# Two transformer blocks on one core: MoBA key rotation in three parts, second block's keys inside the fourth feed-forward, compressed second layer over qg's first unit

## The chip, the cores and the metric

The kernel runs on one core of a Trainium2 chip. The metric is the device time of one execution in microseconds. TensorE multiplies, VectorE (DVE) and ScalarE (ACT) work on tiles, GpSimd (POOL) makes inverse roots, and SyncE (SP) issues the weights' DMAs. Each engine runs its own instructions in the order in which they were written, and waits on semaphores for the others.

## The reference, cut to what matters

The first block mixes DSA attention (indexer, top-64 keys) with MoBA attention (one block of 256 here, so plain causal attention) and a gated feed-forward. The second block has four feed-forwards, a short convolution, and NSA attention, whose keys and values are made from the stream between the two layers:

```python
k_b = apply_rope(rms_norm(k_b.reshape(B, S, MOBA_HEADS, HEAD_DIM), g_k_moba[l]), cos_h, sin_h)
...
kv = (_rmsnorm(h, kv_norm) @ kv_w).reshape(b, s, N_KV_SLOTS, N_KV_GROUPS, HEAD_DIM_2)
k_cmp = _rmsnorm(_compress(kv[0], cmp_pos[0], cmp_w1[0], cmp_b1[0], cmp_w2[0]), k_norm[0])
v_cmp = _compress(kv[1], cmp_pos[1], cmp_w1[1], cmp_b1[1], cmp_w2[1])
k_sel = _rmsnorm(kv[2], k_norm[1])...
k_win = jnp.pad(_rmsnorm(kv[4], k_norm[2]), pad)
...
def _compress(x_raw, pos, w1, b1, w2):
    ...
    return jax.nn.gelu(flat @ w1 + b1) @ w2
```

There are 256 tokens, a model width of 1024, and everything is float32.

## The kernel before

**Weights.** All weight matrices are cut into units of 128 x 2048 words. A ring of three slots takes them from memory. ScalarE rounds a unit into its high half (`w_hi`, L926, and L1216 inside a feed-forward), VectorE subtracts for the low half (`w_lo`, L1264, which also frees the raw slot for the next DMA), and TensorE makes each product from three matmuls: high x high, high x low, low x high (L1741 to L1743). One part of a projection is one unit: 24 matmuls of 512 columns, two token tiles times four slices of the depth. The activations have halves too (`h_hi` L988, `h_lo` L1406), made from transposed tiles of x (L1908).

**Order.** `make_plan` writes one list of items by hand; every engine walks it and does its share of each item, so a place in the list is a place in five queues. `part(stage, chunk, number, parts, after, inside)` puts the items of `inside` between the quarters or halves of a unit's matmuls and those of `after` behind them, and then the split of the unit three further on (unless `held`). `tp` is a group of transposes into bank 6 or 7, in turn, with its copy out; `evac` takes a product out of its banks. `t_free` and `t_done` count the groups.

**First block.** The stages run qi, ki, qb, kb, vb, ga, and so on. The indexer's score goes in eight `ix` items (two matmuls at L1979, two relus on ScalarE at L1138, two scaled additions on VectorE at L1549; each waits for the one before). At the evacuation of kb, ScalarE copies and squares, and VectorE makes the tables, sums the squares (L1492), rotates both token tiles (`rope`, L1277 to L1280, four operations each) and scales by the inverse root (L1504). The item `tp kb` transposes the keys behind vb's second unit (L1914). MoBA attention runs between the quarters of ga (`qk` L1993, `sm`, transposes of the probabilities L1962, `pv`).

**Second block.** kv makes six slots in three chunks: chunk 0 for the compressed branch, chunks 1 and 2 for selected and windowed keys and values. `keys(c)` on VectorE scales the keys with root and gain and writes them twice (L1307, L1309), into `kp` and `kd`, one buffer for both chunks. `kvt` groups transpose them (L1939, copy L1032): chunk 1's in front of the fourth feed-forward, `f3`, chunk 2's between the two compressed layers. `cm` makes the hidden rows of the compressed keys and values (two units each), their evacuation is a GELU (L1115), `hc` transposes them, `cmp` multiplies by the second layer (L2007 and L2011), and `kc` transposes the compressed key. Then come qg (queries), gn (gates) and the NSA attention, in which ScalarE's exponentials (L1170) and VectorE's maxima (L1593) and scalings (L1609) pass work to TensorE pair by pair.

**Feed-forward.** `ffn` has 11 steps. A step multiplies two gate/up units, then the down unit of the step before, then transposes the gated activations. Steps 0 to 2 and 9 to 10 are written out, six run in a loop. `square` (L956) makes the norm's sums of squares.

## Time and profile before

| | |
|---|---|
| median of three runs | 1521.61 us (1521.04 to 1523.71) |
| the profiled execution | 1521.8 us, span 1519.8 us |
| TensorE busy | 1465.2 us, 96% |
| VectorE busy | 851.5 us, 56% |
| ScalarE busy | 689.8 us, 45% |
| DMA, mean | 178 GB/s, q1 at 53.6% of 16 engines |
| mean granted TensorE clock | 0.987 |

The page gives the busy time of each engine over the whole span. The timeline gives, for each group of equal instructions, its start, its length, and in brackets how long its engine stood idle before it and what ended that. The windows view adds the granted TensorE clock of a stretch, as a share of 2.4 GHz. Matmuls overlap, so a distance between two starts prices them better than their length.

### The profile page before, as it was taken

Reading aid. Unit: us, or ns where it says so; the run is one execution under the profiler, and the core shown is the slowest. Engines: PE = TensorE matmul, PEld = TensorE weight load, DVE = VectorE, ACT = ScalarE, POOL = GpSimd, SP = SyncE. Lnnn points to the kernel's source line nnn. Section 1 sums busy time; section 2 is a strip of 40 time slices with the busy share of each in tenths; the row PEclk is TensorE's granted clock in tenths of the full one; section 3 lists DMA queues with packets and bytes.
Section 4 is the critical chain, followed back from the end, with each engine's and each line's share of the span. In section 5 each row is a group of like instructions: output and inputs, shape, how many; then the busy total and the mean of one; then the engine's idle time right before and its main releaser. Section 6 shows DMA issues by size and latency. Waiting matters only on the chain.

```text
span 1519.8 us, 18042 instructions
## 1 busy us (share of the span) xinstructions
PE 1465.2 (96%) x6944; PEld 1168.5 (77%) x6944; DVE 851.5 (56%) x1032; ACT 689.8 (45%) x875; POOL 37.4 (2%) x53
## 2 busy tenths in 40 slices
PE   6989999999999999999999999989999988999998
PEld 3747777788888888888888888778888765788887
DVE  2676765555446544456755545565554567654453
ACT  2535453443344444454453444654344575554432
POOL 0010100000000000000000000210000020000000
PEclk9999999999999999999999999999999998999999
DMA  9853754465554665546555555555556430355562
GB/s 339 284 188 111 253 190 166 166 203 188 190 194 138 222 193 178 183 159 202 192 175 185 193 186 174 146 186 191 179 191 193 145 111 1 95 183 192 176 192 77
DMA packets 187880, 270.11 MB, mean 178 GB/s; under 512 B 8350, under 2 KB 134118, under 8 KB 187816
## 3 DMA queue, kind: packets, MB, share of 16 engines
q1 hardware_dynamic: 186448, 267.01, 53.6%
q10 hardware_dynamic: 1208, 1.94, 0.4%
q0 software_dynamic: 160, 0.26, 0.2%
q8 instruction: 44, 0.72, 0.2%
q14 instruction: 20, 0.16, 0.0%
HBM read 268.15 MB, written 1.05 MB: 177 GB/s over the span
## 4 chain that ended last, share of the span: by engine, by line
PE 85%; DVE 6%; ACT 4%; DMA 2%; issue 2%; SPq 1%; POOL 0%; ACTq 0%; DVEq 0%
PE bank L1741 25%; PE bank L1743 25%; PE bank L1742 25%; DVE w_lo_ring L1264 2%; PE bank L1771 2%; ACT w_hi_ring L926 2%; PE bank L1879 1%; DMA arena<-in_w_mod_dram 1%; PE bank L1908 1%; PE bank L2063 1%; PE bank L1966 1%; DMA raw_ring<-in_w_in_dram 1%; SPq L830 0%; PE bank L2042 0%; DVE h_lo L1406 0%
## 5 line engine op out<-in xcount | busy, mean ns | idle before, releaser
L1264 DVE TENSOR_TENSOR w_lo_ring<-raw_ring,w_hi_ring 128x2048 fp32r<-128x2048 f32 (+1 forms) x228 | 518.4, 2277 | 420.3 <-ACT w_hi_ring L1216 332.4
L1741 PE MATMUL bank<-w_hi_ring,h_hi 128*128 128x512 f32 x1360 | 544.6, 400 | 6.1 <-DVE h_lo L1406 3.1
L1743 PE MATMUL bank<-w_hi_ring,h_lo 128*128 128x512 f32 x1360 | 532.4, 391 | 0.0
L1742 PE MATMUL bank<-w_lo_ring,h_hi 128*128 128x512 f32 x1360 | 532.1, 391 | 0.0
L1216 ACT ACTIVATE w_hi_ring<-raw_ring 128x2048 fp32r<-128x2048 f32 x158 | 302.8, 1916 | 295.8 <-PE bank L1743 293.6
L1741 PEld LDWEIGHTS bank<-w_hi_ring,h_hi 128*128 128x128 f32 x1360 | 256.6, 189 | 75.8 <-issue 24.6
L1743 PEld LDWEIGHTS bank<-w_hi_ring,h_lo 128*128 128x128 f32 x1360 | 256.5, 189 | 55.4
L1742 PEld LDWEIGHTS bank<-w_lo_ring,h_hi 128*128 128x128 f32 x1360 | 257.0, 189 | 49.7
L1741 PE MATMUL bank<-w_hi_ring,f_hi 128*128 128x512 f32 (+1 forms) x456 | 177.4, 389 | 0.0
L1743 PE MATMUL bank<-w_hi_ring,f_lo 128*128 128x512 f32 (+1 forms) x456 | 176.5, 387 | 0.0
L1742 PE MATMUL bank<-w_lo_ring,f_hi 128*128 128x512 f32 (+1 forms) x456 | 176.2, 386 | 0.0
L926 ACT ACTIVATE w_hi_ring<-raw_ring 128x2048 fp32r<-128x2048 f32 (+2 forms) x70 | 131.1, 1879 | 84.4 <-PE bank L1743 41.5
L1224 ACT ACTIVATE glu_s<-bank,rstd 128x256 f32<-128x256 f32 x88 | 36.9, 471 | 142.0 <-PE bank L1743 142.0
L1741 PEld LDWEIGHTS bank<-w_hi_ring,f_hi 128*128 128x128 f32 (+1 forms) x456 | 85.0, 186 | 17.9 <-issue 1.1
L1743 PEld LDWEIGHTS bank<-w_hi_ring,f_lo 128*128 128x128 f32 (+1 forms) x456 | 85.0, 186 | 17.3
L1742 PEld LDWEIGHTS bank<-w_lo_ring,f_hi 128*128 128x128 f32 (+1 forms) x456 | 85.1, 187 | 16.8
L1691 DVE SCALAR_TENSOR_TENSOR glu_a<-bank,rstd,glu_s 128x256 f32<-128x256 f32 x88 | 38.5, 479 | 64.8 <-ACT glu_s L1224 64.8
L1697 DVE TENSOR_TENSOR f_lo<-bank,f_hi 128x512 fp32r<-128x512 f32 x55 | 37.6, 685 | 10.3 <-ACT f_hi L1230 10.3
L1230 ACT ACTIVATE f_hi<-bank 128x512 fp32r<-128x512 f32 x55 | 32.0, 582 | 20.9 <-PE bank L1771 20.9
L1170 ACT ACTIVATE arena<-bank,mn,arena 128x128 f32<-128x128 f32 (+1 forms) x64 | 31.9, 518 | 10.8 <-DVE mn L1596 10.6
L988 ACT ACTIVATE h_hi<-bank,cols 128x256 fp32r<-128x256 f32 x56 | 21.9, 475 | 31.7 <-PE bank L1908 31.7
L1771 PE MATMUL bank<-const,glu_a 128*128 128x128 f32 x236 | 35.3, 271 | 0.0
(254 smaller groups left out, 881.7 us busy)
## 6 DMA issues: line engine op xcount, KB each, us to landing
raw_ring<-in_ffn_w_gate_up_dram SPq DMA_DIRECT2D x176, 512.0 KB
raw_ring<-in_ffn_w_down_dram SPq DMA_DIRECT2D x44, 1024.0 KB
raw_ring<-in_w_in_dram SPq DMA_DIRECT2D x22, 1024.0 KB
raw_ring<-in_w_gate_up_dram SPq DMA_DIRECT2D x44, 512.0 KB
arena<-in_w_mod_dram SPq DMA_DIRECT2D x12, 1024.0 KB, 7.8
raw_ring<-in_w_mod_dram SPq DMA_DIRECT2D x12, 1024.0 KB
raw_ring<-in_w_down_dram SPq DMA_DIRECT2D x11, 1024.0 KB
raw_ring<-in_conv_w_in_dram SPq DMA_DIRECT2D x16, 512.0 KB
```

The source lines that it names most:

```text
L926: act.activation(w_hi[:, u % RING, 0:words], raw[:, r % RING, 0:words], ACT.Copy)\
L1170: ins = act.activation(p_n[:, step % 2, 2 * j + br, 0:n], bank[j][:, br * n:br * n + n], ACT.Exp, scale=rqp[:, qt, h:h + 1], bias=mn[:, c: ...
L1216: act.activation(w_hi[:, u % RING, :], raw[:, unit_raw[u] % RING, :], ACT.Copy)\
L1224: act.activation(glu_s[:, tt, :], glu_bank(f, jb, tt)[:, 0:GC], ACT.Silu, scale=rstd[:, tt:tt + 1] if f else 1.0).then_inc(sem("sg_ready"), 1)
L1230: act.activation(f_hi[:, jb % 2, :, :].rearrange("p a b -> p (a b)"), bank[6 + tg % 2][:, :], ACT.Copy).then_inc(sem("hi_t"), 1)
L1264: dve.tensor_tensor(w_lo[:, u % RING, 0:words], raw[:, r % RING, 0:words], w_hi[:, u % RING, 0:words].bitcast(F32), ALU.subtract).then_inc ...
L1691: dve.scalar_tensor_tensor(glu_a[:, tt, :], glu_bank(f, jb, tt)[:, GC:2 * GC], rstd[:, tt:tt + 1] if f else 1.0, glu_s[:, tt, :], ALU.mult ...
L1697: dve.tensor_tensor(f_lo[:, jb % 2, :, :].rearrange("p a b -> p (a b)"), bank[6 + tg % 2][:, :], f_hi[:, jb % 2, :, :].rearrange("p a b -> ...
L1741: pe.matmul(dst, hi, whi, start=start, stop=False)
L1742: pe.matmul(dst, hi, wlo, start=False, stop=False)
L1743: return pe.matmul(dst, lo, whi, start=False, stop=stop)
L1771: ins = pe.transpose(bank[6 + tg % 2][:, kk * T + tt * P:kk * T + (tt + 1) * P], glu_a[:, tt, kk * P:(kk + 1) * P], ident)
```

## The change

**MoBA keys.** At the evacuation of kb VectorE now only makes the tables and sums the squares. The rest is in three new items, `rot` for each token tile and `rot scale`, which stand inside vb: behind the last quarter of its first unit (after `ix` 5), behind the first quarter of its second unit, and behind its last quarter. The index items move back by a quarter where needed, and `tp kb` moves into ga, behind its first quarter.

**Keys of the second block.** `kp` and `kd` get a second buffer each. `keys(1)` moves from the evacuation of kv 1 to step 0 of `f3`, ahead of `keys(2)`. The four groups of key transposes stand in step 2 of `f3`, two between its gate/up units and two behind them, and ScalarE's copies stand ahead of and behind its silu. The evacuation of kv 2 waits for the sums of squares of kv 1 in place of the keys.

**Compressed branch.** The second layer of the compressed keys (`cmp` 0), their root and transposes, and the second layer of the values stand between the quarters of qg's first unit; the squares of the norm come behind that unit. The split that followed qg's second unit stands behind gn's evacuation and two query copies, ahead of the gates' transposes.

```diff
-        part("gn", 0, 0, 1, [evac("gn"), tgroup("qn", 2, c=0), one("tp", stage="gnt", g=0)])
+        part("gn", 0, 0, 1, [evac("gn"), tgroup("qn", 2, c=0), one("then split", unit=len(units) - 1), one("tp", stage="gnt", g=0)])
...
-    part("vb", 0, 0, 2, [mod_row(6, 1)], [index[3], [], index[4], index[5]])
-    part("vb", 0, 1, 2, [mod_sum(6), tgroup("kb", 2), evac("vb")], [index[6], [], index[7], []])
+    rot = [[dict(kind="rot", tt=tt)] for tt in range(TT)] + [[dict(kind="rot scale")]]
+    part("vb", 0, 0, 2, [mod_row(6, 1)], [[], index[3], index[4], index[5] + rot[0]])
+    part("vb", 0, 1, 2, [mod_sum(6), evac("vb")], [rot[1], index[6], index[7], rot[2]])
...
-    part("ga", 0, 0, 2, [topk(0, 0)], inside[0])
+    part("ga", 0, 0, 2, [topk(0, 0)], [tgroup("kb", 2) + inside[0][0]] + inside[0][1:])
...
-    begin_glu("f3", 6, FIRST_PAIR[3], tgroup("norm", 4, norm=6)[2:] + [dict(kind="square")] + kvt(1, 2))
+    begin_glu("f3", 6, FIRST_PAIR[3], tgroup("norm", 4, norm=6)[2:] + [dict(kind="square")])
...
-    part("cm", 0, 1, 2, [kvt(2, 2), evac("cm", 0)])
-    part("cm", 1, 0, 2, [[dict(kind="square")]])
-    part("cm", 1, 1, 2, [evac("cm", 1)], [[dict(kind="tp", stage="hc", g=0, c=0), dict(kind="cmp", s=0)], []])
-    part("qg", 0, 0, 2, inside=[[dict(kind="tp", stage="kc", g=0), dict(kind="tp", stage="hc", g=0, c=1)], [],
-                                [dict(kind="cmp", s=1)], []])
-    part("qg", 0, 1, 2, [evac("qg", 0)])
+    part("cm", 0, 1, 2, [evac("cm", 0)])
+    part("cm", 1, 0, 2)
+    part("cm", 1, 1, 2, [evac("cm", 1)], [[dict(kind="tp", stage="hc", g=0, c=0)], []])
+    part("qg", 0, 0, 2, [[dict(kind="square")]], [[dict(kind="cmp", s=0)], [dict(kind="tp", stage="hc", g=0, c=1)],
+                                                  [dict(kind="tp", stage="kc", g=0)], [dict(kind="cmp", s=1)]])
+    part("qg", 0, 1, 2, [evac("qg", 0)], held=True)
...
+        kps = (kp, carve(TT, 256))
+        kds = (kd, kv_d_flat[:, 0:1024].rearrange("p (t g u d) -> p t g u d", t=TT, g=NG, u=2))
...
-                            act.wait_ge(sem("kd_done"), 1)
+                            act.wait_ge(sem("qss_ready"), item["nq"])
...
+                        def key_copies(c):
+                            for a in item["keys"] if jb == 2 else ():
+                                if a["c"] == c:
+                                    act.wait_ge(sem("t_done"), a["tg"] + 1)
+                                    act.activation(kn_t[:, c - 1, 2 * a["g"]:2 * a["g"] + 2, :].rearrange("p a b -> p (a b)"),
+                                                   bank[6 + a["tg"] % 2][:, :], ACT.Copy).then_inc(sem(f"t_free{a['tg'] % 2}"), 1)
...
-                        if c == 1:
-                            keys(c)
...
+                if k == "rot":
+                    tt = item["tt"]
+                    dve.wait_ge(sem("t_done"), find["tg", "qb", 1] + 1)
+                    rope(ro[:, tt, :], pq[:, tt, :], tab_c[:, tt, :], tab_s[:, tt, :], NH, HD)
+                if k == "rot scale":
+                    dve.wait_ge(sem("qr_ready"), key_nq + 1)
...
-                            (lambda: keys(2), compressed_operand, lambda: compressed_operand_lo(0))[j]()
+                            (lambda: (keys(1), keys(2)), compressed_operand, lambda: compressed_operand_lo(0))[j]()
...
+                    def key_transposes(c):
+
+                        for a in item["keys"]:
+                            if a["c"] == c:
+                                wait_bank(pe, a["tg"])
+                                pe.wait_ge(sem("kd_done"), c)
+                                for kk in range(2):
+                                    for tt in range(TT):
+                                        at = T * kk + P * tt
+                                        ins = pe.transpose(bank[6 + a["tg"] % 2][:, at:at + P],
+                                                           kds[c - 1][:, tt, 2 * a["g"] + kk, :, :].rearrange("p a b -> p (a b)"), ident)
...
+                        if jb == 2:
+                            key_transposes(1)
                         glu_unit(u + 1, 1, None, two).then_inc(sem("unit_used"), 1)
+                        if jb == 2:
+                            key_transposes(2)
```

## Rows read from the trace of the kernel before

**Rows 1.** The page, busy time of each engine with its share of the span and instructions.

```profile
PE 1465.2 (96%) x6944; PEld 1168.5 (77%) x6944; DVE 851.5 (56%) x1032; ACT 689.8 (45%) x875; POOL 37.4 (2%) x53
```

**Rows 2.** The waits of TensorE: us in total, times, longest us.

```profile
PE bank L1966 <- DVE arena L1609: 3.9, 3, 1.7
```

**Rows 3.** Timeline, VectorE near 100: start, us, instruction, count, idle before.

```profile
94.12 0.68 DVE L1277 TENSOR_TENSOR glu_s<-arena 128x512 f32<-128x512 f32 x1
...
98.36 1.29 DVE L1504 TENSOR_TENSOR arena<-arena,qr 128x512 f32<-128x512 f32 x2
99.57 2.28 DVE L1264 TENSOR_TENSOR w_lo_ring<-raw_ring,w_hi_ring 128x2048 fp32r<-128x2048 f32 x1
101.77 0.80 DVE L1549 SCALAR_TENSOR_TENSOR arena<-arena 128x128 f32<-128x128 f32 x2
...
104.72 1.07 DVE L1549 SCALAR_TENSOR_TENSOR arena<-arena 128x256 f32<-128x256 f32 x2 [1.03 <-ACT arena L1138]
```

**Rows 4.** Timeline, TensorE from 100 to 124.

```profile
103.04 1.22 PE L1979 MATMUL bank<-arena 64*128 64x256 f32 x4 [5.67 <-ACT arena L1138]
...
115.27 1.07 PE L1914 MATMUL bank<-const,arena 128*128 128x128 f32 x8
...
123.06 0.30 PE L1962 MATMUL bank<-const,arena 128*128 128x128 f32 x1 [0.57 <-ACT arena L1145]
```

**Rows 5.** Windows: length, PE, PEld, DVE, ACT, POOL busy, clock, DMA share, GB/s.

```profile
97.40:103.00 5.60, 0.00 (x0) 0.00 (x0) 5.37 (x8) 0.77 (x2) 0.00 (x0) 0.88 0.01 3
103.00:108.40 5.40, 5.36 (x18) 2.53 (x18) 3.77 (x6) 2.46 (x3) 0.00 (x0) 0.50 0.58 191
...
990.00:997.00 7.00, 4.71 (x26) 3.70 (x27) 5.90 (x11) 4.49 (x8) 3.80 (x2) 1.00 0.92 309
1194.60:1198.10 3.50, 0.33 (x3) 0.19 (x2) 1.77 (x2) 3.42 (x6) 0.89 (x2) 0.90 0.23 31
1198.10:1204.40 6.30, 6.30 (x25) 5.08 (x25) 3.69 (x7) 0.79 (x3) 0.72 (x2) 0.51 0.88 296
...
1244.00:1300.00 56.00, 49.73 (x294) 32.09 (x293) 40.53 (x103) 32.56 (x111) 4.44 (x3) 0.88 0.00 1
```

**Rows 6.** Timeline, TensorE in front of the fourth feed-forward.

```profile
990.76 0.47 PE L1741 MATMUL bank<-w_hi_ring,h_hi 128*128 128x512 f32 x1 [3.13 <-DVE h_lo L1406]
...
996.04 1.44 PE L1939 MATMUL bank<-const,arena 128*128 128x128 f32 x8 [1.40 <-DVE h_lo L1406]
...
997.24 0.48 PE L1741 MATMUL bank<-w_hi_ring,h_hi 128*128 128x512 f32 x1
...
1000.08 0.39 PE L1741 MATMUL bank<-w_hi_ring,h_hi 128*128 128x512 f32 x1
```

**Rows 7.** Timeline, VectorE at kv and in step 2 of f3.

```profile
983.07 0.43 DVE L1307 TENSOR_TENSOR arena<-arena,qr 128x256 f32<-128x256 f32 x1 [2.05 <-POOL qr L861]
...
985.34 4.48 DVE L1264 TENSOR_TENSOR w_lo_ring<-raw_ring,w_hi_ring 128x2048 fp32r<-128x2048 f32 x2
...
1033.95 2.29 DVE L1264 TENSOR_TENSOR w_lo_ring<-raw_ring,w_hi_ring 128x2048 fp32r<-128x2048 f32 x1 [2.88 <-ACT w_hi_ring L1216]
```

**Rows 8.** Timeline, TensorE in the compressed branch and at gn.

```profile
1188.31 1.44 PE L1939 MATMUL bank<-const,arena 128*128 128x128 f32 x8 [0.47 <-DVE h_lo L1406]
...
1198.10 0.68 PE L2007 MATMUL bank<-arena 128*60 128x64 f32 x4 [3.18 <-ACT arena L1042]
...
1221.06 0.32 PE L1919 MATMUL bank<-const,arena 48*128 48x48 f32 x2 [1.37 <-ACT arena L1036]
```

**Rows 9.** Timeline, ScalarE behind qg's first chunk.

```profile
1218.35 1.93 ACT L926 ACTIVATE w_hi_ring<-raw_ring 128x2048 fp32r<-128x2048 f32 x1
...
1223.18 1.91 ACT L926 ACTIVATE w_hi_ring<-raw_ring 128x2048 fp32r<-128x2048 f32 x1
...
1227.58 1.28 ACT L1170 ACT_TABLE_LOAD   x1 [2.49 <-DVE arena L1585]
```

More of the change, by code:

```diff
@@ L462, in make_plan @@
             item["tg"], item["hl"], item["gi"] = number("tg", NJ), number("hl", NJ), number("gi", NJ)
+            item["keys"] = [dict(c=c, g=g, tg=item["tg"] + 2 + 2 * (c - 1) + g) for c in (1, 2) for g in range(2)] if item["f"] == 3 else []
+            number("tg", len(item["keys"]))
             for u in range(item["have"], min(item["unit"] + 3 * NJ + RING, len(units))):
@@ L728, in wait_product, with act_group @@
             eng.wait_ge(sem("unit_used"), find["unit", stage, chunk] + 1)
+        def act_group(item, jb):
+            return item["tg"] + jb + (len(item["keys"]) if jb >= 2 else 0)
         def glu_bank(f, jb, tt):
@@ L1023, in _ @@
                         act.activation(ki_t, b[:, 0:T], ACT.Copy).then_inc(free, 1)
-                    elif st == "kvt" and item["c"] == 0:
+                    elif st == "kvt":
                         s_, g0 = divmod(2 * g, NG)
@@ L1030, in _ @@
                            .then_inc(free, 1)
-                    elif st == "kvt":
-                        act.activation(kn_t[:, item["c"] - 1, 2 * g:2 * g + 2, :].rearrange("p a b -> p (a b)"),
-                                       b[:, :], ACT.Copy).then_inc(free, 1)
                     elif st == "qn":
@@ L1930, in _ @@
                     elif st == "kvt":
-                        if item["c"] == 0:
-                            wait_pair(pe, find["pi", "kv", 0])
-                            s_, g0 = divmod(2 * g, NG)
-                            srcs = [kv_d[:, tt, s_, g0 + kk, :, :] for kk in range(2) for tt in range(TT)]
-                        else:
-                            pe.wait_ge(sem("kd_done"), item["c"])
-                            srcs = [kd[:, tt, 2 * g + kk, :, :] for kk in range(2) for tt in range(TT)]
+                        wait_pair(pe, find["pi", "kv", 0])
+                        s_, g0 = divmod(2 * g, NG)
+                        srcs = [kv_d[:, tt, s_, g0 + kk, :, :] for kk in range(2) for tt in range(TT)]
                         for q, s_ in enumerate(srcs):
@@ L2104, in step @@
                             if jb == NJ - 1 and kk == 0:
-                                glu_transposes(item["tg"] + jb, item["gi"] + jb)
+                                glu_transposes(act_group(item, jb), item["gi"] + jb)
                         ins.then_inc(sem("unit_used"), 1)
                         if jb < NJ - 1:
-                            glu_transposes(item["tg"] + jb, item["gi"] + jb, two, 0 if i is None else i)
+                            glu_transposes(act_group(item, jb), item["gi"] + jb, two, 0 if i is None else i)
                     free_pairs(item)
@@ L2120, in _ @@
                     body, q = item["of"], item["q"]
-                    u, tg = body["unit"] + 3 * NJ - 1, body["tg"] + NJ - 1
+                    u, tg = body["unit"] + 3 * NJ - 1, act_group(body, NJ - 1)
                     nb, tt = divmod(q, 2)
```

37 lines of the change are left out of this document (26 added, 11 removed).

## The prediction

> **What bounds the kernel now.** Read the engine totals first: TensorE is busy 1465.2 of 1519.8 us [rows 1]. Everything else hides behind it, so an edit is worth only the TensorE idle time it removes, the half-speed time which that idle brings, and the TensorE work it adds or saves. So next comes TensorE's timeline, for its gaps, and behind each gap the queue of the engine named as releaser. Three gaps lie where the diff works.
>
> First, at 103.04 TensorE stood 5.67 us for a relu [rows 4]. VectorE explains it: from 94.12 it made the MoBA key rotation (two ropes, then the scaling at 98.36), then a weight split at 99.57, and only at 101.77 the indexer sum that lets the relu go [rows 3]. After the gap the granted clock is 0.50, that is 1.2 GHz, from 103.0 to 108.4, where it had been 2.4 GHz [rows 5]. Second, at 990.76 TensorE stood 3.13 us for h_lo, and at 996.04 again 1.40 us [rows 6]; VectorE made kv's first keys at 983.07 and behind them two splits of 4.48 us before h_lo [rows 7]. Third, at 1198.10 it stood 3.18 us for the hidden row's transposed copy [rows 8]; ScalarE was busy 3.42 of these 3.50 us with squares and a split that stand ahead of the copy, and the clock was then 0.51 to 1204.4 [rows 5].
>
> **A. Rotation in three parts.** VectorE is free at 94.1; the high half of the pending split is ready about 94.65 (ScalarE's like piece takes 1.93 [rows 9]). Its new queue: split 2.28 to 96.9; third index sum 0.80 to 97.7. The hand-off from that sum over relu to TensorE is 103.04 - 102.57 = 0.47 [rows 3, 4], so index product 5 runs at 98.2 instead of 103.04. TensorE comes to it at about 97.1 (its work ended by 97.4 [rows 5], and one wait of 0.3 on its way goes with the new order), so a wait of 1.1 remains. VectorE goes on: two index sums of 1.07 with 0.45 of hand-off, rot 2.1 (94.12 to 98.36 is two of them), a 128x512 addition 0.68, split 2.28, rot 2.1, two index sums 2.14, scaling 1.29 [rows 3]. Sum 97.7 + 13.2 = 110.9: only then may the key transposes run. TensorE's work from product 5 to the old key transposes is 115.27 - 103.04 = 12.2 [rows 4], of which 5.4 ran at half speed and so holds 2.7 [rows 5]; without that it is 9.5, and TensorE comes to ga at 107.7. The transposes now stand behind ga's first quarter, two triples of three products at 0.71 (997.24 to 1000.08 is four [rows 6]), so from 109.1 it waits 1.8. From there to the first probability transpose at 123.06 the order is the old one, with 0.57 idle that goes, since VectorE and ScalarE have their splits behind them. Work from 103.04 to 123.06: 20.0 - 0.57 - 2.7 = 16.7; new 98.2 + 16.7 + 1.8 = 116.7, gain 6.3. I take **6.0** for hand-offs unpriced. Bounds: 4 if the new wait costs a piece of low clock as the old one did and VectorE is a little late, 8.4 (5.67 + 2.7) if no wait is left.
>
> **B. kv and the fourth feed-forward.** Keys 1 leave VectorE's queue ahead of the splits (983.07 to 985.34 and the wait for the root before it). The first split can start at 981.65, when its high half is done; two splits of 2.24 end at 986.15, the first two h_lo, half of four of like size, at 987.0. TensorE ends kv at 987.5, so the 3.13 gap goes whole: 3.3 by starts. Then two runs of four triples (2.84 each) and eight transposes bring it to the first unit of the feed-forward at 994.0; there it needs the third h_lo, whose queue (evacuation of kv 2, split 2.28, h_lo 0.85) ends at 994.95. So 994.95 stands against 1000.08 [rows 6]: 5.1. What moves into step 2: 16 transposes. Eight take 1.07 busy [rows 4], of which some 0.24 lies over their neighbours (996.04 + 1.44 against 997.24); the old ones took 1.20 start to start [rows 6]. I take 0.8, so 1.6, and 2.4 as the upper bound. A TensorE transpose, per the Trainium skill (TensorE: Matmul & The Clock Gate, Part 4: PE-mode transpose), took some 275 ns in the context of one kernel; by that the 16 would cost 4.4 us and the total would be 2.8 us worse; the rows here show 0.13 busy for each and decide against it. Behind them: step 0 now carries both keys on VectorE, 2.3 more ahead of three splits; the second unit of step 1 would be split at 1022.9, needed at 1028. In step 2 ScalarE copies two key groups (1.1) before its next split. The low half of that unit ends at 1036.24 [rows 7], and would end 1.1 later; TensorE asks for it 1.6 later too, at 1041.1 in old time. The weights' DMAs are issued when the low halves are done, so at most 2.3 later once, with more than a step of cover. No loss from either, up to 3 us if this cover fails. Net **3.5** (1 to 4.3).
>
> **C. Compressed branch.** The key transposes of kv 2 leave (wait 0.47 and 1.37 start to start, with edges 2.0). The hidden row is evacuated right behind the first compressed layer, 1.4 earlier than the table load now lets it, and the squares leave the queue ahead of its copy. ScalarE: evacuation 1188.1 to 1189.75, split to 1191.6, split to 1194.1 (0.6 allowed for its weights to land), copy 1194.3; TensorE asks at 1195.75, because qg's first quarter now stands before the product. The 3.18 gap goes, and the half-speed time to 1204.4, whose 5.9 up to the next transposes hold 2.8 of loss [rows 5]. The root of the compressed key now has two qg quarters over it: sums, root and scaling, 2.1 us, end at 1199.1; TensorE asks at 1199.2. One wait of 0.25 comes in front of the second half of the second layer, for VectorE's split. 2.0 + 3.2 + 2.8 - 0.25 = **7.8**. Bounds: 5 if the clock falls anyway or the root is 1 us late, 8.5.
>
> **D. The split of qg's last unit.** It moves behind gn's evacuation and two query copies. TensorE's 1.37 wait at 1221.06 [rows 8] falls to 0.2. But the attention behind it is led by ScalarE and VectorE: exp loads its table at 1227.58 on VectorE's word, which follows the split that ScalarE ended at 1225.1 [rows 9]. Before, that stretch of ScalarE had no idle; now it waits 0.35 for gn, 0.35 for transposes, while no work leaves it. So the chain starts 0.7 later, and TensorE, though 1.2 us ahead, waits for it: three waits for the scaled probabilities make 3.9 [rows 2]. **-0.7** (+1.2 to -1.5).
>
> **Sum.** 6.0 + 3.5 + 7.8 - 0.7 = 16.6. The profiled execution took 1521.8, its span 1519.8 with 2.0 around it, and the median is 1521.6, the same within 0.2. 1521.8 - 16.6 = 1505.2; I say **1505**.
>
> **Rivals.** (1) *The waits stay, smaller, and the clock falls.* The new 1.8 in A, and 1.0 to 2.0 in front of the attention's first products, bring stretches at 1.2 GHz; the old ones in the attention bring its mean to 0.88 [rows 5]. One in A costs 1.7, one in D 1.7: 1508.5. For it: 3.18 at 1198.10 brought one. Against it: 3.13 and 1.40 at 990.76 and 996.04 brought none, the clock stayed 1.00 [rows 5]. Chance 0.2. (2) *VectorE stays late in A, or the copies hold ScalarE in step 2.* A gives 2.5 or B loses 3: 1508 to 1510. VectorE's queue from 94.65 to 110.9 has almost no air; each us more is one us less gain. Chance 0.13. (3) *The attention gets better.* 0.88 over 56 us is some 13 us at half clock, 6.7 of loss [rows 5]; a shift of the whole kernel may spare part: 4 spared, 1501. Chance 0.1. (4) *Slower.* In the attention TensorE is busy 49.73 of 56 us [rows 5]. With the chain later and TensorE ahead its waits lengthen; if the clock then stays at 1.2 GHz through the stage, each us of work costs another. It eats the gain from 33 us of wall time at half clock on, and over the whole stage costs some 40: 1545. For it, 0.88 already; against it, total work is the same and the waits grow under 2 us. Chance 0.03. The Trainium skill (TensorE: Matmul & The Clock Gate, HAM oscillation) tells of a kernel in which recurring waits throttle the array again at each tile; by that rule case 4 would come. (5) *The change doesn't move the path*, because what I call released is held by another wait: near 1520, 0.03. The forecast itself, 0.51.
>
> **Range and chances.** 1500 to 1511 holds the forecast, (1), (2) and most of (3). A measurement tells 0.2%, 3 us, from no change. Faster 0.94, same 0.03, slower 0.03.
>
> **What would show it.** In the changed profile: the wait before the fifth index product about 1 us and one of 1 to 2.5 before the key transposes; clock 1.00 at 98 to 108; no gap over 0.5 before the fourth feed-forward's first product and about 1 before its first unit; 16 more transposes in it and no gap in its steps 2 and 3; no gap over 1 and full clock in the compressed layers; the exp table load 0.7 later behind qg's evacuation than now. It is wrong if TensorE stands over 3 us at the key transposes, if step 3 waits for a split, or if the attention takes more than 2 us longer from qg's evacuation to its end.

## The result and the profile after

The changed kernel takes 1504.36 us in the median of four runs (1503.17 to 1506.15), against 1521.67 before (1521.04 to 1523.71). The ratio is 0.9888, with a 95% interval of 0.9875 to 0.9900. Its profiled execution took 1503.4 us with a span of 1501.4, so it is 18.4 us shorter than that of before. A later set of five runs of the same kernel gave 1504.62.

Engine totals of the changed kernel, as in [rows 1]:

```profile
PE 1458.0 (97%) x6944; PEld 1164.5 (78%) x6944; DVE 850.9 (57%) x1032; ACT 689.9 (46%) x875; POOL 36.2 (2%) x53
```

The instructions are as many as before. TensorE's busy time fell by 7.2 us, though its work is the same, because less of it ran at half clock. The other 11 us are idle time that is gone.

**Part A.** Timeline of VectorE in the changed kernel (start, us, instruction, idle before), against [rows 3]:

```profile
95.68 2.29 DVE L1284 TENSOR_TENSOR w_lo_ring<-raw_ring,w_hi_ring 128x2048 fp32r<-128x2048 f32 x1 [0.44 <-ACT w_hi_ring L940]
97.89 0.80 DVE L1580 SCALAR_TENSOR_TENSOR arena<-arena 128x128 f32<-128x128 f32 x2
...
101.32 0.68 DVE L1297 TENSOR_TENSOR glu_s<-arena 128x512 f32<-128x512 f32 x1
...
110.53 1.28 DVE L1562 TENSOR_TENSOR arena<-arena,qr 128x512 f32<-128x512 f32 x2
```

Timeline of TensorE in the changed kernel, against [rows 4]:

```profile
99.16 0.70 PE L2006 MATMUL bank<-arena 64*128 64x256 f32 x4 [0.75 <-ACT arena L1149]
...
111.96 1.07 PE L1945 MATMUL bank<-const,arena 128*128 128x128 f32 x8 [1.44 <-DVE arena L1562]
...
124.57 0.30 PE L1989 MATMUL bank<-const,arena 128*128 128x128 f32 x1 [1.40 <-DVE arena L1611]
```

The index sum stands ahead of the rotation now. Behind the 5.67 us the kernel before had two more waits, 0.57 at 123.06 [rows 4], which is gone, and this one, for which the row at 124.57 stands now:

```profile
129.23 0.30 PE L1962 MATMUL bank<-const,arena 128*128 128x128 f32 x1 [0.56 <-DVE arena L1580]
```

So 6.80 us of waits (5.67, 0.57, 0.56) have become 3.59 (0.75, 1.44, 1.40). The windows view of the changed kernel (length, busy time of PE, PEld, DVE, ACT and POOL, clock, DMA share, GB/s) shows full clock behind the first, where [rows 5] had 0.50, at the fourth feed-forward and in the compressed branch, and 0.94 in the attention:

```profile
99.20:104.60 5.40, 5.40 (x29) 3.11 (x30) 4.61 (x10) 2.56 (x4) 0.00 (x0) 1.00 0.57 189
...
984.00:991.00 7.00, 5.93 (x31) 4.75 (x30) 4.44 (x7) 5.88 (x10) 2.73 (x4) 1.00 0.42 136
1186.00:1198.00 12.00, 12.00 (x63) 9.36 (x62) 6.64 (x12) 5.78 (x16) 1.62 (x4) 1.00 0.72 259
1228.00:1284.00 56.00, 49.62 (x306) 31.95 (x306) 42.97 (x108) 35.13 (x119) 4.44 (x3) 0.94 0.00 1
```

**Parts B and C.** TensorE in the changed kernel, against [rows 6] and [rows 8]: the first unit of the fourth feed-forward, the key transposes in its step 2, the first compressed product and the gates' transposes.

```profile
988.86 0.47 PE L1772 MATMUL bank<-w_hi_ring,h_hi 128*128 128x512 f32 x1 [1.07 <-DVE h_lo L1426]
...
1017.13 1.04 PE L2121 MATMUL bank<-const,arena 128*128 128x128 f32 x8
1017.92 0.48 PE L1772 MATMUL bank<-w_hi_ring,h_hi 128*128 128x512 f32 x1
...
1186.72 0.43 PE L2034 MATMUL bank<-arena 128*60 128x64 f32 x4
...
1203.56 0.32 PE L1950 MATMUL bank<-const,arena 48*128 48x48 f32 x2 [0.25 <-ACT arena L1047]
```

**Part D.** ScalarE in the changed kernel, against [rows 9]: the first line is the evacuation of qg's first chunk, from which the attention's start is counted below.

```profile
1199.68 0.69 ACT L1135 ACTIVATE arena<-bank,rstd 128x512 f32<-128x512 f32 x1 [4.25 <-PE bank L1774]
...
1203.88 1.92 ACT L940 ACTIVATE w_hi_ring<-raw_ring 128x2048 fp32r<-128x2048 f32 x1
...
1211.90 1.28 ACT L1181 ACT_TABLE_LOAD   x1 [2.49 <-DVE arena L1616]
```

**A ledger.** Both kernels issue the same 1848 high x high matmuls in the same order, so the start of the k-th in one trace can be set against the k-th in the other ("product" below means such a matmul). How far the changed kernel is ahead:

| at | ahead, us | step |
|---|---|---|
| 64th, before the first index wait | -1.1 | first loads of the run |
| 87th, behind the last wait of A | 4.7 | **A: +5.7** |
| 204th, near 240 us | 6.3 | +1.6: a half-clock stretch of before, from 238.2 us, is absent |
| first product of f3's first unit | 11.2 | **B, waits: +4.95** |
| behind f3's step 2 | 9.4 | **B, 16 transposes: -1.8** |
| evacuation of qg's first chunk | 16.4 | **C: +7.0** |
| first product of the attention's fifth pair | 15.7 | **D: -0.7** |
| first product of wo | 18.4 | +2.7: fewer half-clock stretches in the attention |

### The profile page after: what moved, and what is told of

It reads as the page before. It is cut to its first block, busy times and chain, and to the rows that moved or that the text cites. A ratio compares the mean times of both kernels' runs of the same rounds, so it can differ in the third digit from the quotient of the medians.

```text
span 1501.4 us, 18041 instructions
## 1 busy us (share of the span) xinstructions
PE 1458.0 (97%) x6944; PEld 1164.5 (78%) x6944; DVE 850.9 (57%) x1032; ACT 689.9 (46%) x875; POOL 36.2 (2%) x53
## 4 chain that ended last, share of the span: by engine, by line
PE 87%; DVE 5%; ACT 3%; DMA 2%; issue 2%; SPq 0%; POOL 0%; DVEq 0%; ACTq 0%
PE bank L1772 26%; PE bank L1774 26%; PE bank L1773 26%; PE bank L1802 2%; DVE w_lo_ring L1284 2%; ACT w_hi_ring L940 1%; PE bank L1910 1%; PE bank L1939 1%; PE bank L2090 1%; DMA raw_ring<-in_w_out_dram 1%; DMA raw_ring<-in_w_in_dram 1%; DMA arena<-in_w_mod_dram 1%; PE bank L1993 1%; PE bank L1922 0%; PE bank L2069 0%
## 5 line engine op out<-in xcount | busy, mean ns | idle before, releaser
L1774 PEld LDWEIGHTS bank<-w_hi_ring,f_lo 128*128 128x128 f32 (+1 forms) x456 | 84.7, 186 | 17.3
```

Source lines behind the costliest of these rows:

```text
L1774: return pe.matmul(dst, lo, whi, start=False, stop=stop)
```

## The experiments

Each stands on the changed kernel, and each median is set beside that of the kernel before on the same chip: 1520.99 for the first four, 1523.21 for the next four, 1522.34 for the last four.

### One part undone at a time

**Rotation in one piece again (A undone).**

```diff
...
-    part("vb", 0, 0, 2, [mod_row(6, 1)], [[], index[3], index[4], index[5] + rot[0]])
-    part("vb", 0, 1, 2, [mod_sum(6), evac("vb")], [rot[1], index[6], index[7], rot[2]])
+    part("vb", 0, 0, 2, [mod_row(6, 1)], [index[3], [], index[4], index[5]])
+    part("vb", 0, 1, 2, [mod_sum(6), tgroup("kb", 2), evac("vb")], [index[6], [], index[7], []])
...
-    part("ga", 0, 0, 2, [topk(0, 0)], [tgroup("kb", 2) + inside[0][0]] + inside[0][1:])
+    part("ga", 0, 0, 2, [topk(0, 0)], inside[0])
...
```

> The changed kernel with the MoBA key rotation put back in one piece at the evacuation of kb, and its key transposes back behind vb. Queue theory (each part's worth is the TensorE wait that it removes, with the half-speed time behind it, and the parts add up): the 5.67 us wait and about 5 us at 1.2 GHz come back, 5.6 to 6.3 us more than the changed kernel, so about 1509.5 to 1510. Rival, clock theory (a good part of the whole gain is where the half-speed stretches happen to fall, in the attention and elsewhere, and moves with any shift): anything from +2 to +9, with stretches at 1.2 GHz in other places of the attention than in the changed kernel.

Measured: 1510.33 us, ratio 0.9926 (0.9904 to 0.9947), 6.0 above the changed kernel. Timeline of TensorE and windows of this kernel:

```profile
103.50 0.80 PE L2002 MATMUL bank<-arena 64*128 64x256 f32 x2 [5.67 <-ACT arena L1148]
```

```profile
103.40:109.00 5.60, 5.50 (x18) 2.53 (x18) 3.97 (x6) 2.51 (x4) 0.00 (x0) 0.50 0.57 185
```

The same 5.67 and the same half clock behind it are back. By the ledger between this kernel and the changed one it loses 5.8 us from the 64th product to the 87th: this is A, by itself, against 5.7 between the kernel before and the changed one. Near 240 us this trace has a half-clock stretch again (clock 0.85 from 234 to 241), which costs it 1.7 more.

**Second block's keys in their old places (B undone),** the copies and waits with them.

```diff
-    begin_glu("f3", 6, FIRST_PAIR[3], tgroup("norm", 4, norm=6)[2:] + [dict(kind="square")])
+    begin_glu("f3", 6, FIRST_PAIR[3], tgroup("norm", 4, norm=6)[2:] + [dict(kind="square")] + kvt(1, 2))
...
-    part("cm", 0, 1, 2, [evac("cm", 0)])
+    part("cm", 0, 1, 2, [kvt(2, 2), evac("cm", 0)])
```

> The kernel before with the rotation, the compressed branch's order and the moved split, but with the second block's keys made and transposed where they were (chunk 1 in front of the fourth feed-forward, chunk 2 between the compressed layers, one buffer). Queue theory: the 3.1 and 1.4 us waits in front of the fourth feed-forward come back, 16 transposes leave it (1.8), and 1.8 to 2.0 us of key transposes with their wait stand in the compressed branch again: 5.1 us more than the changed kernel, about 1509. Rival: VectorE's splits in front of the feed-forward were covered anyway and only the 16 transposes move: within 1.5 us of the changed kernel.

Measured: 1510.54 us, ratio 0.9932 (0.9914 to 0.9950), 6.2 above. Timeline of TensorE and windows of this kernel:

```profile
984.45 0.47 PE L1755 MATMUL bank<-w_hi_ring,h_hi 128*128 128x512 f32 x1 [3.15 <-DVE h_lo L1407]
...
989.73 1.44 PE L1953 MATMUL bank<-const,arena 128*128 128x128 f32 x8 [1.41 <-DVE h_lo L1407]
```

```profile
984.00:997.00 13.00, 11.02 (x55) 8.95 (x56) 6.58 (x11) 8.09 (x12) 4.69 (x4) 1.00 0.64 216
```

Both waits are back to 0.02 us, and again without any fall of the clock. The ledger goes down by 5.1 us from kv to f3's first unit, back by 1.8 at step 2, and down by 1.8 again between the compressed layers, where the second chunk's transposes now stand. So these last 1.8, which the prediction booked under C as "2.0", need B.

**Compressed branch in its old order (C undone).**

```diff
-    part("cm", 1, 0, 2)
-    part("cm", 1, 1, 2, [evac("cm", 1)], [[dict(kind="tp", stage="hc", g=0, c=0)], []])
-    part("qg", 0, 0, 2, [[dict(kind="square")]], [[dict(kind="cmp", s=0)], [dict(kind="tp", stage="hc", g=0, c=1)],
-                                                  [dict(kind="tp", stage="kc", g=0)], [dict(kind="cmp", s=1)]])
+    part("cm", 1, 0, 2, [[dict(kind="square")]])
+    part("cm", 1, 1, 2, [evac("cm", 1)], [[dict(kind="tp", stage="hc", g=0, c=0), dict(kind="cmp", s=0)], []])
+    part("qg", 0, 0, 2, inside=[[dict(kind="tp", stage="kc", g=0), dict(kind="tp", stage="hc", g=0, c=1)], [],
+                                [dict(kind="cmp", s=1)], []])
```

> The changed kernel with the compressed branch's old order (second layer of the keys between the halves of the first layer's last unit, squares ahead of it), the key transposes staying in the feed-forward. Queue theory: TensorE comes 2 us earlier but the hidden row's copy too, since ScalarE has no key copies; it still stands behind squares and a split: a wait of about 3 us and 6 us at 1.2 GHz come back, 5 to 5.7 us more than the changed kernel, about 1509. Rival: the key transposes and copies in that place were what made the wait; with them gone it is under 1 us and the clock stays, 1505 to 1506.

Measured: 1507.64 us, ratio 0.9915 (0.9892 to 0.9938), 3.3 above. Timeline of TensorE and windows of this kernel:

```profile
1187.11 0.43 PE L2034 MATMUL bank<-arena 128*60 128x64 f32 x4 [2.54 <-ACT arena L1053]
...
1191.43 0.24 PE L1979 MATMUL bank<-const,arena 60*128 60x60 f32 x1 [0.96 <-DVE arena L1691]
```

```profile
1187.10:1193.40 6.30, 5.34 (x32) 4.37 (x33) 3.61 (x7) 2.23 (x12) 0.73 (x2) 1.00 0.90 303
```

The two waits make 3.5 and the ledger 3.1. The half-clock stretch that I had tied to the wait did not come back: behind 2.54 us the clock stayed at 2.4 GHz, behind the 3.18 us of before it fell [rows 5]. So C alone is worth 3.1, with the transposes of B 4.9, and the other 2.1 of the 7.0 comes of the half-clock stretch and of the longer wait that the profiled execution of before had there. From the first compressed product to the transpose of the compressed key the same instructions take 5.92 us there (1198.10 to 1204.02) and 3.36 here without the wait (1187.11 to 1190.47). Half clock thus cost 2.6, but it covered the 0.96; 1.6 is left of it, and the wait was 0.6 longer. Why one wait brought half clock and the other didn't is not shown.

**Squares late, product early (half of C undone).**

```diff
-    part("cm", 1, 1, 2, [evac("cm", 1)], [[dict(kind="tp", stage="hc", g=0, c=0)], []])
-    part("qg", 0, 0, 2, [[dict(kind="square")]], [[dict(kind="cmp", s=0)], [dict(kind="tp", stage="hc", g=0, c=1)],
+    part("cm", 1, 1, 2, [evac("cm", 1)], [[dict(kind="tp", stage="hc", g=0, c=0), dict(kind="cmp", s=0)], []])
+    part("qg", 0, 0, 2, [[dict(kind="square")]], [[], [dict(kind="tp", stage="hc", g=0, c=1)],
```

> Half of part C undone: the squares of the queries stay behind the qg unit, but the first compressed product stands again behind its transposes, not a quarter of the qg unit later. Theory: of the 2.54 us wait that the kernel without C has at 1187 us, the squares ahead in ScalarE's queue are about half, so a wait of about 1.3 us on ScalarE's copy ahead of the first product is back, and the ledger is 1.3 us (up to 1.6) short of the changed kernel there, less than the 3.25 us of the kernel without C. Rival 1: the squares are all of it, no wait over 0.4 and no loss. Rival 2: the squares are none of it, the 2.54 us are back.

Measured: 1508.39 us, ratio 0.9900 (0.9874 to 0.9926). Timelines of TensorE and ScalarE of this kernel:

```profile
1185.77 0.43 PE L2034 MATMUL bank<-arena 128*60 128x64 f32 x4 [1.57 <-ACT arena L1053]
```

```profile
1183.65 1.91 ACT L940 ACTIVATE w_hi_ring<-raw_ring 128x2048 fp32r<-128x2048 f32 x1 [1.13 <-DMA raw_ring<-in_nsa_w_qg_dram]
1185.46 0.25 ACT L1053 ACTIVATE arena<-bank 128x120 f32<-128x120 f32 x1
```

1.57 of the 2.54 us are back, and the ledger is 1.4 short, so neither rival holds: the squares are worth 0.97, the product's place behind a quarter of qg 1.57. The wait ends on the copy, but the copy stood behind a split that began 1.13 us late for its weights. The releaser that the row names is the last link, not the cause. The total is 4 us above the changed kernel, more than the wait; the profiled execution had 0.88 of clock in the attention, which comes below.

**Split of qg's last unit in its old place (D undone).**

```diff
-        part("gn", 0, 0, 1, [evac("gn"), tgroup("qn", 2, c=0), one("then split", unit=len(units) - 1), one("tp", stage="gnt", g=0)])
+        part("gn", 0, 0, 1, [evac("gn"), tgroup("qn", 2, c=0), one("tp", stage="gnt", g=0)])
...
-    part("qg", 0, 1, 2, [evac("qg", 0)], held=True)
+    part("qg", 0, 1, 2, [evac("qg", 0)])
```

> The changed kernel with the split of qg's last unit back right behind the evacuation of qg's first chunk. My step D: the attention is led by ScalarE and VectorE, so TensorE's 1.2 us wait at the gates' transposes comes back and costs nothing, and the exponential's table is loaded 0.7 us earlier after qg's evacuation (11.5 in place of 12.2): 0.7 us less than the changed kernel. Rival: TensorE's own queue leads: 1.2 us more than the changed kernel.

Measured: 1505.98 us, ratio 0.9897 (0.9880 to 0.9915). Timelines of ScalarE and TensorE of this kernel:

```profile
1200.42 0.69 ACT L1135 ACTIVATE arena<-bank,rstd 128x512 f32<-128x512 f32 x1 [4.26 <-PE bank L1774]
...
1211.94 1.28 ACT L1181 ACT_TABLE_LOAD   x1 [2.49 <-DVE arena L1616]
```

```profile
1205.43 0.32 PE L1950 MATMUL bank<-const,arena 48*128 48x48 f32 x2 [1.37 <-ACT arena L1047]
```

TensorE's wait of 1.37 is back, and the exp table load stands 11.52 us behind the evacuation (1211.94 - 1200.42), 0.7 less than the 12.22 of the changed kernel (1211.90 - 1199.68). The fifth pair's first product comes at 27.43 against 28.13, also 0.7. So the mechanism is right. Whether the split is better in its old place cannot be told from the totals: they differ by 1.6 us the other way and their ranges overlap (1504.72 to 1507.26, 1503.17 to 1506.15).

### Prices and what leads

**Key transposes issued twice.**

```diff
-                                for kk in range(2):
+                                for kk in [0, 1] * 2:
                                     for tt in range(TT):
```

> The changed kernel, but the key transposes that part B put into the fourth feed-forward's second step are issued twice each (16 transposes of 128 by 128 more, into the same places, so the output is the same). It prices the disputed term of B. Theory (0.1 to 0.11 us for one, from the 0.8 to 0.9 us that eight take start to start): the second step is longer by 1.6 to 1.8 us, and the time by as much (about 1506.1). The Trainium skill's figure of about 275 ns for one (TensorE: Matmul & The Clock Gate, Part 4) would make it 4.4 us longer (about 1508.8). Rival: the banks or ScalarE's copies out of them hold TensorE, and it is about 3 us, with waits that end on ScalarE between them.

Measured: 1510.20 us, ratio 0.9917 (0.9900 to 0.9933). Timeline of TensorE of this kernel:

```profile
1017.93 1.91 PE L2121 MATMUL bank<-const,arena 128*128 128x128 f32 x16
1019.60 0.48 PE L1772 MATMUL bank<-w_hi_ring,h_hi 128*128 128x512 f32 x1
```

Start to start, sixteen transposes take 1.67 us where eight took 0.79 (1017.13 to 1017.92), so one more costs 0.11. The second group gives the same 1.67, and no wait stands near: 1.76 us for all 16, as the theory said. The source view of the changed kernel gives the length of one (ns, least, median, most):

```profile
L2121 PE MATMUL bank<-const,arena x16: 270/272/273, 1017.1 to 1024.2; 128*128 128x128 f32 x16
```

The Trainium skill's 275 ns (TensorE: Matmul & The Clock Gate, Part 4: PE-mode transpose), given for bfloat16, agrees with this length. But in a group each starts 0.11 us behind the one before, so 16 times the length is not the price. The total, though, rose by 5.8 us, and it did so in each of the four executions (1509.25 to 1510.59). In the profiled one, 4.7 of the 7.2 us by which it is later at the end arise in the attention, where its clock was 0.88 against 0.94, though nothing in it was edited. So a total would have priced these transposes at three times their cost.

**Key transposes of A one product later.**

```diff
-    part("ga", 0, 0, 2, [topk(0, 0)], [tgroup("kb", 2) + inside[0][0]] + inside[0][1:])
+    part("ga", 0, 0, 2, [topk(0, 0)], [inside[0][0], tgroup("kb", 2), inside[0][1] + inside[0][2], inside[0][3]])
```

> The changed kernel, but in part A the second key block's transposes stand one product later in the gate stage (behind the rotation's second part, not ahead of it). Nothing is left out. It tests what the 1.44 us wait at 111.96 (prediction: 1.8) is: VectorE's rotation of the keys coming late for transposes that have nothing that needs them so soon. Theory: the wait falls to about 0.2, and the time by 1.2 to 1.3 us against the changed kernel (about 1503.1). Rival: the wait goes to whoever needs the transposed keys next (the scores' first transposes), total 0.3 us or less.

Measured: 1503.93 us, ratio 0.9876 (0.9860 to 0.9893). Timeline of TensorE of this kernel:

```profile
111.96 1.06 PE L1945 MATMUL bank<-const,arena 128*128 128x128 f32 x8
```

The first MoBA scores, which need the transposed keys, move back by a quarter of ga's unit too. The transposes start at 111.96 as in the changed kernel, but without the wait: a quarter of ga's unit has run in its place. The next wait, 1.40 at 124.57 in the changed kernel, is 1.39 at 123.19, so nothing was passed on, and TensorE is 1.4 earlier. The total shows 0.4 of it, with 0.88 of clock in the attention of the profiled execution.

**First output unit's split behind the attention's first maxima.**

```diff
-        part("gn", 0, 0, 1, [evac("gn"), tgroup("qn", 2, c=0), one("then split", unit=len(units) - 1), one("tp", stage="gnt", g=0)])
-        part("qg", 1, 0, 2, inside=[one("nsa", c=0) + pair(-1), pair(0)])
+        part("gn", 0, 0, 1, [evac("gn"), tgroup("qn", 2, c=0), one("then split", unit=len(units) - 1), one("tp", stage="gnt", g=0)], held=True)
+        part("qg", 1, 0, 2, inside=[one("nsa", c=0) + pair(-1) + one("then split", unit=len(units) - 1), pair(0)])
```

> The changed kernel with one edit more: the split of the first attention output unit (that ScalarE and VectorE do ahead of the second layer's attention) stands behind the attention's first maxima instead of ahead of them. Nothing is left out of the computation. It tests the last step of part D: what leads the attention's first exponentials. Theory: the instructions between the second layer's last qg evacuation and the first exp on ScalarE lead, so with about 2.4 us of them gone the exp table load comes about 2.3 us earlier after that evacuation than in the changed kernel (9.8 to 10.0 in place of 12.22 us), the first product of the fifth pair about as much earlier on TensorE (25.7 to 26.0 in place of 28.13), and the time falls by about 2.3 us, to about 1502. Rival: TensorE's own list leads (or ScalarE's sum of work, which is the same), then the pair comes earlier by 0.5 us or less and the time stays at 1504.

Measured: 1504.44 us, ratio 0.9876 (0.9860 to 0.9892). Timeline of ScalarE of this kernel:

```profile
1199.43 0.69 ACT L1135 ACTIVATE arena<-bank,rstd 128x512 f32<-128x512 f32 x1 [4.25 <-PE bank L1774]
...
1207.25 1.91 ACT L940 ACTIVATE w_hi_ring<-raw_ring 128x2048 fp32r<-128x2048 f32 x1
1209.18 1.28 ACT L1181 ACT_TABLE_LOAD   x1
```

The load comes at 9.75 behind the evacuation and the fifth pair at 25.68, 2.47 and 2.45 earlier, as the theory said: the VectorE chain behind that split led the attention. With 2.49 us of idle gone, ScalarE's own queue leads. But wo starts at 83.04 behind the evacuation, where the changed kernel has 81.11. What was gained by the fifth pair was given back before wo; the clock in this stretch was 0.90 in this execution, against 0.94.

**Both edits.**

```diff
...
-        part("qg", 1, 0, 2, inside=[one("nsa", c=0) + pair(-1), pair(0)])
+        part("qg", 1, 0, 2, inside=[one("nsa", c=0) + pair(-1) + one("then split", unit=len(units) - 1), pair(0)])
...
-    part("ga", 0, 0, 2, [topk(0, 0)], [tgroup("kb", 2) + inside[0][0]] + inside[0][1:])
+    part("ga", 0, 0, 2, [topk(0, 0)], [inside[0][0], tgroup("kb", 2), inside[0][1] + inside[0][2], inside[0][3]])
```

> The changed kernel with both edits: the key transposes of part A one product later, and the first output unit's split behind the attention's first maxima. Theory: the two savings lie on the path at different places (112 us and 1225 us) and add up: 1.2 to 1.3 plus 2.3, so about 3.5 us below the changed kernel (about 1500.9). Rival: one of them is lost to a wait further on (then 1502 to 1503).

Measured: 1503.32 us, ratio 0.9871 (0.9854 to 0.9887). The load stands at 9.74 and the wait at 112 us is gone, so both waits go in one kernel. But its profiled execution has a half-clock stretch behind the 1.77 us wait near 232 us (clock 0.84 from 234 to 241), which takes 2.1 us back, and 0.90 of clock in the attention. The median is the lowest of all kernels here, 1.0 below the changed kernel and not the 3.5 forecast, and the intervals overlap: it can't be told from the changed kernel by time.

### The attention's clock

**The changed kernel once more.**

> The changed kernel itself, once more. In its first profile 10.2 us of the second layer's attention (1216 to 1280 us) had a granted clock of half, in the five other kernels with the same work in that stretch 13.6 to 20.5 us, though the waits in it are the same. Theory (that part of the time is the execution's luck and not the kernel's): this profile shows another set of half-clock stretches in the attention with waits within 0.1 us of those of the first, and the median lies within 2 us of 1504.4. Rival (the places of the waits decide it, and so each kernel has its own sum): the same stretches within 1 us and the time at 1504.4.

Measured: 1504.62 us, ratio 0.9883 (0.9862 to 0.9903). Windows from the evacuation to wo's first product, first of the changed kernel, then of the same kernel again, of C undone, of both edits and of the transposes later:

```profile
1199.68:1280.79 81.11, 70.96 (x420) 46.55 (x419) 57.86 (x135) 54.60 (x159) 9.02 (x6) 0.94 0.16 52
```

```profile
1200.02:1282.85 82.83, 71.39 (x421) 46.75 (x419) 57.77 (x135) 54.62 (x159) 9.01 (x6) 0.94 0.15 51
```

```profile
1203.45:1283.86 80.41, 69.67 (x420) 45.48 (x419) 57.59 (x135) 54.50 (x159) 9.01 (x6) 0.96 0.16 53
```

```profile
1200.15:1283.32 83.17, 74.23 (x421) 49.34 (x419) 57.90 (x135) 54.57 (x159) 9.00 (x6) 0.90 0.15 51
```

```profile
1198.69:1284.15 85.46, 75.58 (x420) 50.19 (x419) 57.67 (x135) 54.60 (x159) 9.02 (x6) 0.88 0.15 50
```

Work is the same in all five: 420 or 421 TensorE instructions, 57.8 us of VectorE, 54.6 of ScalarE. What varies is the clock, and the length follows it: 80.41 us at 0.96, 81.11 and 82.83 at 0.94, 85.46 at 0.88. The kernels of the transposes issued twice (85.77) and of half of C (85.46) have 0.88 too, those of A and B undone 0.94 (82.74 and 82.13). With the half-clock time taken as 2 x (1 - clock) x length, the eight profiles in which this stretch was not edited lie within 1 us of a line of 0.35 us of length for each us at half clock. The theory holds in that the second execution of one kernel is 1.7 us longer with other half-clock stretches, though as much of it in all, and with the same long waits (2.04 for the 2.05 at 1222.75, 1.68 for the last, at 1274.29). Windows of the first execution and of the second:

```profile
1222.90:1226.40 3.50, 3.50 (x16) 2.46 (x16) 2.86 (x7) 3.50 (x10) 0.00 (x0) 0.51 0.27 94
```

```profile
1232.10:1239.00 6.90, 6.90 (x29) 4.88 (x28) 3.49 (x9) 2.96 (x10) 3.48 (x2) 0.51 0.00 0
```

The stretch at 1222.9, which only the first has, cost nothing: TensorE has waits of 0.25, 0.62 and 1.03 behind the 2.04 in the second, of which one of 0.59 is left in the first, and the fifth pair comes at 28.13 in both. From 1232.1 to 1239.0 TensorE was busy all the time, with no wait to take the slower work. So where a stretch falls counts as well as how long it is. It doesn't follow that all is luck: the kernel with doubled transposes was high in all its executions, and that stays open.

**Filler matmuls in the attention's waits,** in the kernel with both edits.

```diff
-        plan.extend(pair(5) + one("nsa", c=1) + one("cs", tt=0))
-        plan.extend(pair(6) + one("cse", tt=0) + one("cs2", tt=0) + one("cs", tt=1) + hold(5, 5) + pn(2))
-        plan.extend(pair(7) + pc(0) + one("cse", tt=1) + one("cs2", tt=1) + one("nv", step=0))
-        plan.extend(pair(8) + hold(4, 5) + pc(1) + one("nv", step=1) + one("nout", step=0) + pn(3))
+        plan.extend(hold(4, 5) + pair(5) + one("nsa", c=1) + one("cs", tt=0))
+        plan.extend(pair(6) + one("cse", tt=0) + one("cs2", tt=0) + one("cs", tt=1) + hold(9, 5) + pn(2))
+        plan.extend(pair(7) + hold(4, 5) + pc(0) + one("cse", tt=1) + one("cs2", tt=1) + hold(5, 5) + one("nv", step=0))
+        plan.extend(pair(8) + hold(4, 5) + pc(1) + hold(3, 5) + one("nv", step=1) + one("nout", step=0) + pn(3))
...
-        plan.extend(pair(12) + pn(5) + one("nout", step=4))
+        plan.extend(pair(12) + hold(7, 4) + pn(5) + one("nout", step=4))
```

> The kernel with both edits (transposes one product later, split behind the first maxima) and 27 filler matmuls of 128 by 256 more in TensorE's waits of the second layer's attention, of the kind that the kernel has there already (10 of them took 2.32 us at full clock); they write parts of banks that nobody reads, so the output is the same. Theory: waits are what the half-clock stretches of the attention follow, so with each wait of over 0.6 us filled the 17.1 us at half clock of its profile fall to 7 or less, which gives back about half the difference, 5 us: about 1498.5. Rival: the stretches come anyway (from the weak activity of the small matmuls between the waits), the fillers take double time in them and hold up the chain: 1504 or more.

Measured: 1506.97 us, ratio 0.9901 (0.9878 to 0.9925). Windows of this kernel over the same stretch:

```profile
1198.59:1282.71 84.12, 80.68 (x475) 56.74 (x473) 57.87 (x135) 54.33 (x159) 9.01 (x6) 0.96 0.15 51
```

Timelines of TensorE near 1244, of the kernel with both edits and of this one:

```profile
1244.48 1.07 PE L1993 MATMUL bank<-const,arena 128*128 128x128 f32 x8 [0.90 <-DVE arena L1640]
...
1247.58 0.63 PE L1983 MATMUL bank<-const,arena 128*128 128x128 f32 x4 [1.07 <-DVE arena L1676]
```

```profile
1244.31 1.89 PE L1833 MATMUL bank<-const 128*128 128x256 f32 x8
1246.04 0.60 PE L1983 MATMUL bank<-const,arena 128*128 128x128 f32 x4
```

The clock rose from 0.90 to 0.96, as the theory wants. But I had read the price wrongly: a float32 filler shows as two instructions (the plan's `hold(5, 5)`, five fillers, is the row "x10" of 2.32 us). Four fillers show as eight and take 1.73 start to start, 0.43 each, where the wait was 1.07. At that price the 27 fillers took 11.7 us for waits of 5.6 (0.90, 1.07, 1.27, 0.69, 1.69); 6.1 more of work against 4.9 less of lost clock (0.10 x 83.2 against 0.04 x 84.1) makes 84.4, and 84.12 was measured. That counts each us at half clock as 0.5; at the 0.35 of above it would be 85.8, so the balance is a rough one. It also explains 0.95 of the 3.65 us between the medians only: the six executions lie between 1502.23 and 1510.72, and where the rest arises is not shown. Fillers of half that number were not tried.

**The same fillers in the changed kernel,** with eight ahead of the second probability transposes.

```diff
-        plan.extend(pair(4) + one("csq") + pn(1))
+        plan.extend(pair(4) + one("csq") + hold(8, 5) + pn(1))
```

> The changed kernel with 31 such filler matmuls in the attention's waits (8 of them ahead of the second transposes of the probabilities, where the wait of 2.05 us at 1222.75 is), and none of the two edits. Theory: the 10.2 us at half clock fall to 3.4 or less, and the time by 1.5 to 3.4 us, to about 1502; the waits are gone from the list and the fifth pair's first product comes at 28.1 us behind the qg evacuation as before. Rival: as for the other, 1504 or more, with the pair later.

Measured: 1510.24 us, ratio 0.9932 (0.9910 to 0.9954). Clock 0.98, stretch 87.86 us, the longest of all. The price was doubled here too, and the eight stood in a place without a wait: the 2.05 us belong to the first probability transposes, one item earlier, and are still there. The fifth pair is at 28.13 as forecast. More clock and more time: a half-clock stretch that TensorE has slack for costs less than the work that keeps it away.

## Why the prediction was right, point by point

The forecast was 1505.0; the median is 1504.4. The terms, against the ledger:

- **A, 6.0 forecast, 5.7 measured.** The waits give 3.2 of it, the clock by difference 2.5 (2.7 forecast). The chain was right link by link: 1.1 forecast before index product 5, 0.75 measured; 1.8 before the key transposes, 1.44; full clock after both. VectorE's scaling ended near 111.8 against 110.9. The 0.57 went, as forecast. Not in the sum was that the wait behind it, 0.56 at 129.23, grows to 1.40 at 124.57, for an attention scaling on VectorE; the prediction had said that VectorE's splits were done by then. The prediction also had the clock at 2.4 GHz up to the end of the 5.67 us; [rows 5] show 0.88 from 97.4 to 103.0, so it fell inside that wait. The undone part gives 5.8.
- **B, 3.5 forecast, 3.15 measured.** The first feed-forward unit came 4.95 earlier (5.1 forecast), with a wait of 1.07 (0.95 forecast, 994.95 less 994.0). The 16 transposes cost 1.8 against 1.6. The upper end of 2.4 is out, and so is 4.4, which took the length of one transpose for its price in a group. Steps 2 and 3 have no wait, so the late copies and splits were covered.
- **C, 7.8 forecast, 7.0 measured.** The wait of 3.2 went as forecast. Each other term was a little too large: the clock's share 2.8 forecast, 2.6 by starts; the transposes 2.0, measured 1.8. The clock's share is also the term least tied to the change, since the wait without C brought no half clock. The wait of 0.25 that the sum took off did not come in the compressed layers, where no wait over 0.2 is left; one of 0.25 stands in front of the gates' transposes, where D had 0.2. By difference some 0.5 is left for the seams of the small products between qg's quarters, which the sum had at nothing.
- **D, -0.7 forecast, -0.7 measured,** by the table load (11.52 to 12.22) and the fifth pair, and confirmed by undoing it. That VectorE's and ScalarE's chain leads there, and not TensorE, is shown by the split moved behind the maxima: 2.45 earlier at the fifth pair.
- **What the sum had at nothing.** The first loads cost 1.1, and half-clock stretches outside the edits gave 4.3 (1.6 near 240 us, 2.7 in the attention). Sum of the four terms by the ledger 15.2, with these 18.4. The forecast of 16.6 thus came out well partly by luck: a shortfall of 1.4 in the parts and a gain of 3.2 beside them lie on opposite sides. Against the medians, 17.3, the terms alone leave 2.1 open.
- **The rivals.** (3), the attention getting better, came in part in the profiled execution: 81.11 against 83.15 us. The second execution of the same kernel, with 82.83, shows most of that as the execution's, and (3)'s price, half of each us at half clock, was too high for this stretch (0.35). (1) is half true: the new waits of A brought no half clock, and the stretch that began behind the 2.05 in the attention cost nothing. (2) is out by the rows of A and step 2. (4) is out: the clock never stayed down, even with TensorE's waits as they were. (5) is out by the undone parts, of which A, B and C lose 6.0, 6.2 and 3.3 us of median, and 5.8, 5.1 and 3.1 by the ledger. With the 1.6 of D the medians add up to 17.1, near the whole of 17.3, but that is luck in part, since in the traces undoing D gains 0.7 up to the fifth pair.

## What to carry to other kernels

Where one engine is 96% busy, price an edit as the wait that it removes minus the wait that its new order creates, by walking the queue of the engine that releases it; here that was within 0.4 us in three of four terms. Check a term of a microsecond or two in the trace, at aligned instructions, and not by the total, which carries several us of clock from elsewhere. Before you fill waits, price the filler from starts, and find which item each wait stands in front of.

## What was not expected of the hardware

- **Waits repeat, half-clock stretches don't.** The 5.67, 3.13, 1.41 and 1.37 us came back within 0.02 in other kernels and other executions. But 3.18 us brought half clock and 2.54 in the same place none, nor did 3.15 at 984 us. A wait of 1.77 near 238 us stands in all 14 profiles and was followed by half clock in three: before, with A undone, and with both edits. The Trainium skill (TensorE: Matmul & The Clock Gate, HAM oscillation) tells of a kernel in which a recurring wait throttles the array again at every tile. Here the same wait does so in some executions only, and the attention's clock lay between 0.88 and 0.96 over the unfilled kernels, so it oscillates, but how often is not set by the list of waits alone. What sets it stays open.
- **Half clock costs less than half.** In the attention a us at half clock cost about 0.35 on the mean of eight profiles, and nothing at 1222.9, since TensorE has waits there that its slower work runs into. In the compressed branch the slow work of before had hidden a later wait of 0.96, which appears only in the kernel at full clock.
